# A streaming encoder step on one core: attention scores kept negated, the sink as a column of each score block, and a new order within the attention slots

## The reference, cut to what matters

```python
s = jnp.einsum('bnqkgd,bnskd->bnkgqs', q, k) * (HEAD_DIM ** -0.5)
s = s - slopes * dist
s = jnp.where(allowed, s, MASK_VALUE)
m = jnp.maximum(jnp.max(s, axis=-1), sink)
p = jnp.exp(s - m[..., None])
denom = jnp.sum(p, axis=-1) + jnp.exp(sink - m)
return jnp.einsum('bnkgqs,bnskd->bnqkgd', p / denom[..., None], v)
```

## Time and profile before

| | |
|---|---|
| median of 3 runs | 1838.98 us (1832.63 to 1844.6) |
| profiled execution, span | 1833.5 us |
| PE busy | 1662.1 us, 91% |
| PE weight load busy | 1358.4 us, 74% |
| DVE busy | 956.3 us, 52% |
| ACT busy | 901.0 us, 49% |
| POOL busy | 807.5 us, 44% |
| mean granted TensorE clock | 0.969 of 2.4 GHz |
| HBM | 85 GB/s over the span |

### The profile page before, as it was taken

How to read it: one execution, slowest core, us unless ns; L and a number is a source line. 1 busy time by engine, 2 the same in 40 slices (tenths; PEclk the granted TensorE clock), 3 DMA queues, 4 the chain that set the end, 5 groups by cost and what they waited for, 6 DMA issues and landing times.

```text
span 1833.5 us, 27902 instructions
## 1 busy us (share of the span) xinstructions
PE 1662.1 (91%) x8843; PEld 1358.4 (74%) x8843; DVE 956.3 (52%) x2191; ACT 901.0 (49%) x1832; POOL 807.5 (44%) x571
## 2 busy tenths in 40 slices
PE   8899899888879899989988899989988899989988
PEld 2777488878879677877777677877777677777767
DVE  2444323666651554367762654367761654367761
ACT  3333223666554434366654444366654543466653
POOL 0322143444345244645555234645555344555544
PEclk9999999999989999999999999999999999999999
DMA  8434543111112333322212433322212323322211
GB/s 273 122 116 130 152 123 104 48 47 48 48 35 70 124 104 98 92 58 58 58 58 69 136 89 98 92 58 59 58 58 73 118 84 102 87 61 60 62 56 69
DMA packets 258678, 158.27 MB, mean 86 GB/s; under 512 B 41007, under 2 KB 242047, under 8 KB 258542
## 3 DMA queue, kind: packets, MB, share of 16 engines
q1 hardware_dynamic: 258542, 156.50, 28.9%
HBM read 147.51 MB, written 9.17 MB: 85 GB/s over the span
## 4 chain that ended last, share of the span: by engine, by line
PE 50%; DVE 21%; ACT 13%; issue 11%; POOL 3%; DMA 2%; SPq 0%; DVEq 0%; ACTq 0%; POOLq 0%
PE ps_u L773 37%; ACT work L1582 4%; DVE work L1305 4%; DVE neg_max L1312 3%; PE ps_o L1007 3%; ACT ps_u L1473 2%; POOL w_lo L1644 2%; PE ps_s L805 2%; PE ps_t L980 2%; DVE ps_u L1149 2%; DVE ps_o L1335 2%; DVE work L1215 2%; DVE acc L1349 1%; ACT w_hi L1384 1%; DVE sink_arg L1313 1%
## 5 line engine op out<-in xcount | busy, mean ns | idle before, releaser
L1644 POOL TENSOR_TENSOR w_lo<-w_raw,w_hi 128x1024 fp32r<-128x1024 f32 (+1 forms) x224 | 520.0, 2323 | 654.4 <-ACT w_hi L1384 621.9
L773 PE MATMUL ps_u<-h_all_hi,w_hi 128*128 128x512 f32 (+2 forms) x1440 | 527.4, 366 | 27.8 <-DVE h_all_lo L1112 8.5
L773 PE MATMUL ps_u<-h_all_lo,w_hi 128*128 128x512 f32 (+2 forms) x1440 | 516.1, 358 | 0.0
L773 PE MATMUL ps_u<-h_all_hi,w_lo 128*128 128x512 f32 (+2 forms) x1440 | 515.7, 358 | 0.0
L773 PEld LDWEIGHTS ps_u<-h_all_hi,w_hi 128*128 128x128 f32 x1440 | 279.5, 194 | 81.8 <-issue 20.4
L773 PEld LDWEIGHTS ps_u<-h_all_hi,w_lo 128*128 128x128 f32 x1440 | 279.0, 194 | 37.4
L773 PEld LDWEIGHTS ps_u<-h_all_lo,w_hi 128*128 128x128 f32 x1440 | 279.5, 194 | 36.3 <-issue 1.4
L773 PE MATMUL ps_u<-y_hi,w_hi 128*128 128x512 f32 (+1 forms) x640 | 231.4, 362 | 9.4 <-POOL y_lo L1696 7.0
L1384 ACT ACTIVATE w_hi<-w_raw 128x1024 fp32r<-128x1024 f32 (+1 forms) x224 | 227.1, 1018 | 13.0 <-DMA w_raw<-in_pool_w_in_dram 5.9
L773 PE MATMUL ps_u<-y_lo,w_hi 128*128 128x512 f32 (+1 forms) x640 | 228.4, 357 | 0.0
L773 PE MATMUL ps_u<-y_hi,w_lo 128*128 128x512 f32 (+1 forms) x640 | 228.1, 356 | 0.0
(11 more groups left out here) (189 smaller groups left out, 2388.4 us busy)
## 6 DMA issues: line engine op xcount, KB each, us to landing
w_raw<-in_pool_w_in_dram SPq DMA_DIRECT2D x64, 512.0 KB, 3.9
w_raw<-in_attn_w_in_dram SPq DMA_DIRECT2D x64, 512.0 KB, 3.6
x_in<-in_ada_w_dram SPq DMA_DIRECT2D x32, 512.0 KB, 3.8
w_raw<-in_pool_w_out_dram SPq DMA_DIRECT2D x32, 512.0 KB, 3.7
w_raw<-in_attn_w_out_dram SPq DMA_DIRECT2D x32, 512.0 KB, 3.7
x_in<-in_x_prompt_dram SPq DMA_DIRECT2D x16, 512.0 KB, 3.8
w_raw<-in_attn_w_in_dram SPq DMA_DIRECT2D x32, 256.0 KB, 3.2
w_raw<-in_ada_w_dram SPq DMA_DIRECT2D x8, 512.0 KB, 5.6
```

What stands on the lines that cost most here:

```text
L773: last = nc.tensor.matmul(out, w, x, start=(i == 0), stop=(i == n - 1))
L1644: G.tensor_tensor(w_lo[:, j % RING, 0:width[j]], w_raw[:, j % 2, 0:width[j]], w_hi[:, j % RING, 0:width[j]].bitcast(F32), ALU.subtract).th ...
```

## The change

The scores are kept negated. The instruction of line 1305 multiplies by -1/8 instead of 1/8 and takes the minimum instead of the maximum; it starts the minimum from the head's `neg_sink`, a value per partition, instead of from a constant. So it leaves the negated maximum over scores and sink at once. The exponential is called with scale -1. Each block of `work` becomes 260 columns long instead of 256, and ACT writes `neg_sink` into the column just behind the 256 scores (a copy of one element per block, with a wait for its own end), so that the exponential of 257 columns adds the sink's term to the row sum. On DVE the instructions of lines 1312 (neg_max), 1313 (sink_arg) and 1321 (denom) go, with two waits for the engine's own results; those are three small operations per item by the diff. On ACT sink_exp (line 1583) goes. The order in the slot becomes: S, PV, E1, SR, SM, OG, EX, E2, TR, PH, W, YH, PLO, YL. PE's own order doesn't change by that: it has no part in SM, OG or EX.

```diff
-            out += first + to_norm + second
+            out += first + to_norm
+            out += [("SM", a)] if a is not None else []
             out += [("OG", c)] if c is not None else []
+            out += [("EX", a)] if a is not None else []
+            out += second
             out += [("TR", b), ("PH", b)] if b is not None else []
-            out += [("SM", a)] if a is not None else []
             out += [("split",)]
             out += [("YH", c)] if c is not None else []
-            out += [("EX", a)] if a is not None else []
             out += [("PLO", b)] if b is not None else []
             out += [("YL", c)] if c is not None else []
...
-        work = sb("work", [P, 2, 4 * 256])
+        work = sb("work", [P, 2, 4 * BLOCK])
...
-                        last = V.tensor_tensor_reduce(out=out, in0=src, in1=b, scale=HEAD_DIM ** -0.5, scalar=LOWEST, op0=ALU.add,
-                                                      op1=ALU.max, accum_out=row_max[r, d, at:at + 1])
-                    link(last)
-                    h0 = 4 * g + 2 * hp
-                    nt = nb // 2
-                    m2 = lambda x: x[r, d, 0:nb].rearrange("p (t e) -> p t e", e=2)
-                    ns = neg_sink[r, h0:h0 + 2].unsqueeze(1).to_broadcast([r.stop - r.start, nt, 2])
-                    link(V.scalar_tensor_tensor(out=m2(neg_max), in0=m2(row_max), scalar=-1.0, in1=ns, op0=ALU.mult, op1=ALU.min))
-                    V.tensor_tensor(m2(sink_arg), m2(neg_max), ns, ALU.subtract).then_inc(max_ready, 1)
+                        h = 4 * g + 2 * hp + e
+                        last = V.tensor_tensor_reduce(out=out, in0=src, in1=b, scale=-HEAD_DIM ** -0.5, scalar=neg_sink[r, h:h + 1],
+                                                      op0=ALU.add, op1=ALU.min, accum_out=neg_max[r, d, at:at + 1])
+                    last.then_inc(max_ready, 1)
...
-                    dve.wait_ge(sink_ready, a + 1)
-                    link(V.tensor_tensor(denom[r, d, 0:nb], row_sum[r, d, 0:nb], sink_exp[r, d, 0:nb], ALU.add))
-                    V.reciprocal(recip[r, d, 0:nb], denom[r, d, 0:nb]).then_inc(recip_ready, 1)
+                    dve.wait_ge(exp_ready, a + 1)
+                    V.reciprocal(recip[r, d, 0:nb], row_sum[r, d, 0:nb]).then_inc(recip_ready, 1)
...
+                    end = WINDOW + SAMPLE if it["sample"] else 256
+                    h0 = 4 * it["g"] + 2 * it["hp"]
+                    if a >= 2:
+                        act.wait_ge(p_turned, a - 1)
+                    put = work[r, d, 0:nb * BLOCK].rearrange("p (t e c) -> p t e c", e=2, c=BLOCK)[:, :, :, end]
+                    A(put, neg_sink[r, h0:h0 + 2].unsqueeze(1).to_broadcast([r.stop - r.start, nb // 2, 2]), ACT.Copy).then_inc(sink_put, 1)
+                    act.wait_ge(sink_put, a + 1)
                     act.wait_ge(max_ready, a + 1)
                     if a >= 2:
                         act.wait_ge(recip_ready, a - 1)
                     for at, t, e, k0 in item_blocks(it):
-                        x = work[r, d, at * 256 + k0:at * 256 + (WINDOW + SAMPLE if it["sample"] else 256)]
-                        A(x, x, ACT.Exp, bias=neg_max[r, d, at:at + 1], accum_out=row_sum[r, d, at:at + 1])
-                    A(sink_exp[r, d, 0:nb], sink_arg[r, d, 0:nb], ACT.Exp).then_inc(sink_ready, 1)
+                        x = work[r, d, at * BLOCK + k0:at * BLOCK + end + 1]
+                        last = A(x, x, ACT.Exp, bias=neg_max[r, d, at:at + 1], scale=-1.0, accum_out=row_sum[r, d, at:at + 1])
+                    last.then_inc(exp_ready, 1)
```

More of the change, by code:

```diff
@@ L46 @@
 SHIFT = 2
-LOWEST = -3e38
+BLOCK = 260
 U_PROMPT = 2 * HIST
@@ L475, in trunk_kernel @@
         sinks, neg_sink = sb("sinks", [P, HEADS]), sb("neg_sink", [P, HEADS])
-        row_max, neg_max = sb("row_max", [P, 2, 4]), sb("neg_max", [P, 2, 4])
-        row_sum, sink_arg, sink_exp = sb("row_sum", [P, 2, 4]), sb("sink_arg", [P, 2, 4]), sb("sink_exp", [P, 2, 4])
-        denom, recip = sb("denom", [P, 2, 4]), sb("recip", [P, 2, 4])
+        neg_max, row_sum, recip = sb("neg_max", [P, 2, 4]), sb("row_sum", [P, 2, 4]), sb("recip", [P, 2, 4])
         flat = work[:, :, :].rearrange("p a b -> p (a b)")
@@ L487, in trunk_kernel @@
         hist_rows, mod_rows = bias_flat[0:HIST - 1, :], bias_flat[0:2, :]
-        out_rows = [work[:, 0, :], work[:, 1, :], silu_g[:, :, :].rearrange("p a b -> p (a b)")[:, 0:D_MODEL], bias_flat]
+        out_rows = [work[:, 0, 0:D_MODEL], work[:, 1, 0:D_MODEL], silu_g[:, :, :].rearrange("p a b -> p (a b)")[:, 0:D_MODEL], bias_flat]
         offsets = kv_t[:, 0:2 * WINDOW]
-        landing = [w_raw[:, 0, :], w_raw[:, 1, :], work[:, 0, :], work[:, 1, :], x_in[:, 0, :], x_in[:, 1, :]]
+        landing = [w_raw[:, 0, :], w_raw[:, 1, :], work[:, 0, 0:D_MODEL], work[:, 1, 0:D_MODEL], x_in[:, 0, :], x_in[:, 1, :]]
         c_pairs = c_s[:, :].rearrange("p (v k) -> p k v", v=2)
@@ L530, in trunk_kernel @@
         bias_ready = sem("bias_ready")
-        s_ready, max_ready, exp_ready, sink_ready, recip_ready, norm_ready = (
-            sem("s_ready"), sem("max_ready"), sem("exp_ready"), sem("sink_ready"), sem("recip_ready"), sem("norm_ready"))
+        s_ready, max_ready, exp_ready, sink_put, recip_ready, norm_ready = (
+            sem("s_ready"), sem("max_ready"), sem("exp_ready"), sem("sink_put"), sem("recip_ready"), sem("norm_ready"))
         p_turned, pt_hi_ready, pt_lo_ready, pv_done = (
@@ L974, in _ @@
                                 o = (2 * kt + e) * SAMPLE
-                                src = work[r, a % 2, at * 256 + kt * SAMPLE:at * 256 + kt * SAMPLE + P]
+                                src = work[r, a % 2, at * BLOCK + kt * SAMPLE:at * BLOCK + kt * SAMPLE + P]
                                 last = nc.tensor.transpose(t_flat[:, o:o + SAMPLE], src, ident[r, r])
@@ L979, in _ @@
                                 o = (4 * (at // 2) + 2 * kt + e) * P
-                                last = nc.tensor.transpose(t_flat[:, o:o + P], work[:, a % 2, at * 256 + kt * P:at * 256 + (kt + 1) * P],
+                                last = nc.tensor.transpose(t_flat[:, o:o + P], work[:, a % 2, at * BLOCK + kt * P:at * BLOCK + (kt + 1) * P],
                                                            ident[:, :])
@@ L1299, in _ @@
                         if it["sample"]:
-                            out, src = work[r, d, at * 256:at * 256 + WINDOW + SAMPLE], s_flat[r, at * 256:at * 256 + WINDOW + SAMPLE]
+                            out, src = work[r, d, at * BLOCK:at * BLOCK + WINDOW + SAMPLE], s_flat[r, at * 256:at * 256 + WINDOW + SAMPLE]
                             b = bias[r, 2 * hp + e, 2 * WINDOW - WINDOW - SAMPLE:2 * WINDOW]
                         else:
-                            out, src = work[:, d, at * 256 + k0:at * 256 + 256], s_flat[:, at * 256 + k0:at * 256 + 256]
+                            out, src = work[:, d, at * BLOCK + k0:at * BLOCK + 256], s_flat[:, at * 256 + k0:at * 256 + 256]
                             b = bias[:, 2 * hp + e, k0:256]
-                        last = V.tensor_tensor_reduce(out=out, in0=src, in1=b, scale=HEAD_DIM ** -0.5, scalar=LOWEST, op0=ALU.add,
-                                                      op1=ALU.max, accum_out=row_max[r, d, at:at + 1])
-                    link(last)
-                    h0 = 4 * g + 2 * hp
-                    nt = nb // 2
-                    m2 = lambda x: x[r, d, 0:nb].rearrange("p (t e) -> p t e", e=2)
-                    ns = neg_sink[r, h0:h0 + 2].unsqueeze(1).to_broadcast([r.stop - r.start, nt, 2])
-                    link(V.scalar_tensor_tensor(out=m2(neg_max), in0=m2(row_max), scalar=-1.0, in1=ns, op0=ALU.mult, op1=ALU.min))
-                    V.tensor_tensor(m2(sink_arg), m2(neg_max), ns, ALU.subtract).then_inc(max_ready, 1)
+                        h = 4 * g + 2 * hp + e
+                        last = V.tensor_tensor_reduce(out=out, in0=src, in1=b, scale=-HEAD_DIM ** -0.5, scalar=neg_sink[r, h:h + 1],
+                                                      op0=ALU.add, op1=ALU.min, accum_out=neg_max[r, d, at:at + 1])
+                    last.then_inc(max_ready, 1)
                 elif kind == "SR":
@@ L1702, in _ @@
                     pool.wait_ge(recip_ready, a + 1)
-                    pool.wait_ge(sink_ready, a + 1)
+                    pool.wait_ge(exp_ready, a + 1)
                     r = slice(P - SAMPLE, P) if it["sample"] else slice(0, P)
@@ L1715, in _ @@
                             w = WINDOW + SAMPLE
-                        x = work[r, d, n * 512:n * 512 + 512].rearrange("p (e c) -> p e c", e=2)[:, :, k0:k0 + w]
+                        x = work[r, d, 2 * n * BLOCK:2 * (n + 1) * BLOCK].rearrange("p (e c) -> p e c", e=2)[:, :, k0:k0 + w]
                         last = G.tensor_tensor(x, x, recip[r, d, 2 * n:2 * n + 2].unsqueeze(2).to_broadcast([r.stop - r.start, 2, w]), ALU.mult)
```

## The result

The changed kernel takes 1861.93 us (median, 1857.21 to 1865.16), the one before 1839.78 beside it: ratio 1.013, 95% interval 1.011 to 1.016. It is slower, by 22 us. The profiled execution takes 1860.3 us against 1833.5.

A forecast was written before the change was run, and what follows sets the result against it. PE bounds the kernel, busy 91% of the span, so gains come from its 171 us idle. Three parts give 14 us and part 0 gives 5, together 19: 1839 - 19 = 1820 us, 8-in-10 range 1803 to 1845.

The forecast's parts named there:

- S's waits, neg_max, SM: Between SM and EX: S's waits and gaps go, 2.6 us per part; neg_max was stuck behind POOL; SM takes 1.70 us.
- the 60 ns worked out from the earlier trace: SM's start value read from a tensor: 60 ns more for each of four blocks, 0.24 us per item.
- the rival of a stuck SM: SM locked out behind POOL's instruction, 1.1 us per item coming back: nothing left, 1839 us; chance 0.03.
- The sum: Whole kernel: 4.7 us per part in parts 1 to 3, together 14, plus 5 in part 0: 19 us gained.
- 0.6 per part for VT: VT's wait for KS behind PLO, 1.3 us, shrinks by only 0.2, three times a part: 0.6 us.
- the rival "gives more": PE's clock: half of up to 27 us lost at the lower level comes back, 13 us more: 1807; chance 0.12.
- Weight tiles are split two units ahead, so that 2 us there cost nothing: W, YH, w_lo and YL wait behind EX in a kv slot; the delay of 2 us was priced at nothing.
- My own layout: Kv slot of part 1 from its unit's end: EX 4.6 to 6.6, PH to 7.65, PLO to 8.9 us.
- What DVE saves, PH loses behind EX: Kv slots of part 1: PLO ends at 8.9 us, near where it ended before.
- Behind q0 and in the drain: PV's wait behind q0 grows to 1.4 us, -1.35 per part; the drain comes 1.7 us sooner.
- Part 0: A group takes about 55 us against 57.1 and 56.1, despite new PV waits up to 1.7; 5 us gained.
- The slower rival: EX, SM and TR chained with PH behind: 48 PV waits of 0.9 us, 43 us lost, 1863; chance 0.10.

The follow-up runs named there:

- e11: Changed kernel with only EX put back to its old place behind PH, W and YH: 1771.38 us.
- e7: Changed kernel with TR and PH put ahead of EX, all else as changed: 1789.34 us.
- e3: Changed kernel with the weight-tile split W moved directly behind SR, ahead of SM, OG and EX: 1835.15 us.
- e8: e1 with two dependent small one-input operations (reciprocals nobody reads) put on DVE between SM and max_ready: 1782.26 us.
- e9: e1 with two dependent small two-input operations (minimums nobody reads) put on DVE between SM and max_ready: 1836.67 us, ratio 0.999 to the kernel before.
- e1: Changed arithmetic (negated scores, sink column) with the old slot order, against the kernel before: 1761.33 us, ratio 0.958.
- e4: Changed kernel with the two key copies made by ACT, behind YH: 1841.45 us.
- e10: Changed kernel with POOL making the bias of a group's second head pair one item earlier: 1846.42 us.

## Why the prediction was wrong

Predicted were 1820 us, 1803 to 1845 for 8 times in 10, and 0.12 for slower. Measured were 1862. What failed is that EX, moved ahead of PH, W and YH, was given no price: PH's delay was set off against what DVE saves, and W's was put at nothing. Moving EX back alone returns 91 us (e11), PH ahead of it 73 (e7), W ahead of it 27 (e3). By step:

- **S's waits, neg_max, SM.** That neg_max was stuck behind POOL is confirmed by e8 and e9. S's waits went. SM's line over the whole run after (shortest/median/longest ns):

```profile
L1305 DVE CUSTOM_DVE_ANT_0 work<-ps_s,bias,neg_sink x272: 344/480/485, 329.0 to 1793.6; 128x256 f32<-128x256 f32 x120, 128x128 f32<-128x128 f32 x8, 32x160 f32<-32x160 f32 x8
```

480 ns at the median instead of 420 before, and at most 485: the 60 ns worked out from the earlier trace rows, and never stuck. The Trainium skill ("DVE: scalar operands, raw-bit mode, write accounting and state across instructions", section "1. Scalar operands") says that a value per partition takes up no second input stream; the trace agrees, and the rival of a stuck SM fell. The sink copy on ACT takes 0.20 us; in 53 of 72 items SM ends after it and releases EX, and in 17 EX starts 0.03 us behind it, with SM done already, so there it isn't free.
- **What the removed steps were worth.** The sum had 19 us for change and order together; arithmetic alone is worth 77. Two terms were mis-sized. The sum followed only S's wait on sink_arg. But less work on DVE moves all behind it: in e1 PLO ends 2.1 us sooner in the slots before VT, PV's wait fell by 12.8 us and VT's 11.8 went, where I had 0.6 per part for VT. And in e1 the clock came as the rival "gives more" said, 11 us or more, where I had nothing in the sum; in the changed kernel it went the other way, 0.969 to 0.957.
- **"Weight tiles are split two units ahead, so that 2 us there cost nothing."** This step failed. w_lo comes 4.0 to 4.6 us later in the slots before VT, not 2. My own layout had it: PH ends at 7.65, and W's 1.05 us behind it put w_lo at 8.7, beside a PLO that ends at 8.9, where the earlier trace rows has w_lo at 5.4. That it costs nothing is true of PE, which reads the tiles. It is not true of POOL, which does w_lo, YL and BI in a fixed order: I named w_lo and YL as waiting for W and YH and did not go on to BI, nor from BI to SM. Nor did I ask what DVE does while a w_lo that comes later runs. e4 and e10 show these two omissions to be worth 20 and 16 us, and e3 both of them 27. The 22.5 us by which VT's waits grew are the first.
- **"What DVE saves, PH loses behind EX."** As a reading of parts 1 to 3 this held: PLO ends 0.8 us behind the unit both before and after. (Counted from S it ends at 9.3 to 10.3, against 9.3 to 9.7 before and 8.9 in my layout. EX starts 5.9 us behind S in the slot above, where I had 4.6: PV's new wait of 0.8 us made TR and with it SM late.) What it hides is a price: in e1, with PH ahead of EX, PLO ends 1.3 us before the unit does. With w_lo late beside a PLO no sooner than before, VT's wait, predicted to shrink by 0.2, grew by 2.5, nine times. e7 gives the price of PH's place as 73 us over all parts; my sum set it off against what DVE saves.
- **Behind q0 and in the drain.** PV's wait behind q0 was to grow to 1.4 us; it went, and 0.6 to 0.8 us came in the kv slot in its place. The drain's PV waits, 1.1 and 2.1 in the sum, were 2.1, 2.4 and 0.8. Both are small beside the two steps above.
- **Part 0.** I had 55 us a group. In one turn from long wait to long wait it is 61.3 (415.26 to 476.55), against 57.1 and 56.1 in the earlier trace rows. The three PV waits of up to 1.7 us a group came as predicted (1.6 to 1.7, and a fourth of 1.2); but the long wait, which was to shrink by 1.5, grew by 1.5 to 5.2. What was missing is that SM waits for BI, with PH behind it.
- **The slower rival.** It had "PH stands behind all three", and its time, 1863, is the measured one. Its place is half right: e7 shows that PH's place is worth 73 us. But it expected a PV wait in every slot of parts 1 to 3, and there PV's waits were 6.7 us in part 1, against 5.8. There the price was paid by the key copies, in part 0 by PV. That 1863 fits so well is partly chance.
- **The chance of 0.12** was too low because I priced PH's delay only up to where PLO is needed by PV, and took DVE's other work behind PLO, KS, as if it could only shift, not grow. Nor did it have any row for how long the copies of KS last beside w_lo, since before the change they never met it.

## What to carry to other kernels

Put an instruction that waits behind those that are ready; EX ahead of PH, W and YH gained nothing in any kernel of the study, and while it waited for SM it held up PH, W and YH, which DVE and POOL were waiting for. For each step moved, write down what stands behind it on its own engine, then what stands behind those on the engines that they release, until the list ends or closes to a ring. A small operation with two inputs in SBUF beside a busy GpSimd can last until the GpSimd instruction ends, so count such operations by what runs beside them. And PE's busy time rises with its idle time, in this study by about half of it.

## What the runs showed of the hardware

- A plain 128x128 fp32 copy on DVE took 0.21 us free and 2.27 us when it started 0.16 us after a GpSimd instruction of 2.34 us; with e1's order it takes 0.43 and costs nothing.
- A 128x4 minimum of two inputs took 191 ns at the median, 654 on average and 1982 at most, and a second one behind it 589, 482 and 2285; a 128x4 reciprocal in the same place took 160 to 180 ns.
- The row reduction of 128x256 took 480 ns with its start value read from a tensor, scale and minimum changed with it, against 420 with a constant.
- Per us of idle time that was added, PE's busy time grew by 0.45 us (changed kernel over e1), 0.65 (e7 over e1) and 0.69 (e9 over e8: 24.2 / 35.3); e10 against the changed kernel doesn't follow this.
